# Output projection beside the last HGRN2 head: eight tiles over half of the k-tiles, in place of two tiles over all of them

## The chip, the core and the metric

The kernel runs on one core of one Trainium2 chip. The metric is the device time of one execution, in microseconds. The kernel before takes 3098.37 us (median of 3 runs, 3093.49 to 3100.5).

## What is computed

One decoder layer and a final RMSNorm, for a prompt of 16 meta tokens and 512 tokens, and for 8 sample sequences of 8 tokens (`D_MODEL` 2048, `d_ff` 8192). The parts that matter here:

```
proj = rmsnorm(x) @ w_in                       # 8208 columns, for both head groups
og   = gated DeltaNet, 8 heads (short conv, l2norm, delta rule, head norm, gate)
oh   = HGRN2, 8 heads (state expansion 128):
         f = lb + (1 - lb) * sigmoid(fh);  k = 1 - f
         S_t = diag(f_t) S_{t-1} + k_t v_t^T ;  o_t = S_t^T q_t   (chunks; head norm, gate)
mix  = concat(og, oh)                          # 2048 columns, 128 per head
x    = x + mix @ w_out                         # the output projection and its residual
x    = x + relu(rmsnorm(x) @ w_up)^2 @ w_down
y    = rmsnorm(x)
```

The outputs are y for both groups, and the new conv, DeltaNet and HGRN2 states.

## The kernel before, in words

**Layout.** Activations lie transposed: 128 features on the partitions, tokens along the free dimension (592 = 64 sample + 16 meta + 512 prompt; behind the mixers 576, as two halves of 288). A product of 2048 features is a sum over 16 k-tiles. Each FP32 operand is split into a high part in fp32r (a copy on ScalarE) and a low part (the difference, on VectorE), and a k-tile is three products (high x high, low x high, high x low) of two halves: six matmuls (`ktile`, line 877; its line in the trace is 882). A weight *unit* is eight k-tiles of one output tile (128 x 1024 FP32, 512 KB). It is loaded by SyncE's queue into one of four slots of `w_raw` (`load`, line 490), split by `hi` on ScalarE (A at line 1317) and by `lo` on VectorE (line 1767) into one of two slots of `w_hi` and `w_lo`. A load waits until the low half of the unit four earlier is made; a high half until the unit two earlier is multiplied. Output tiles alternate between two PSUM buffers (`outs`, line 378); a tile may start when the one two earlier has been evacuated (`s_evac`).

**Heads.** For each of the eight heads TensorE runs 16 units of the input projection, and between its k-tiles stages of the mixers: in the first half the HGRN2 stages of the head before, in the second half the DeltaNet stages of this head. So the last HGRN2 head has no input projection left to run beside. Its stages come in the order of `HG_STAGES`: gdn_out, gates, gates_b, turn_v, turn_k, stw, diag, seven levels l1 to l64, o, out, st0. Each engine has its own queue and takes them in this order:

- TensorE (`hg`, line 1091): turn_v and turn_k are transposes (the helper's line is 958), stw the state products (lines 1113 and 1115), diag the diagonal scores (1119), a level 8 or 10 small matmuls (1127), o the outputs (1134 to 1140), out the head norm's sums (942), st0 the sample state (1144).
- VectorE (`hg`, line 2020): gates_b makes the decayed keys `kd` (2048), the first level's argument (1988, 1989) and the products `qe` (2051) and `zs` (2053); turn_k copies the turned keys (2062) and forms the level's operands `q` and `kk` (1998, 1999); stw makes the carried states (2066, 2070); a level takes the scores of the level before (2018, preceded by a one-element instruction of line 145), forms its operands and the argument of the next level but one. Levels wait for each other through these.
- ScalarE (`hg`, line 1463) makes the exponential of each argument (1461).
- GpSimd stores the HGRN2 sample state when VectorE has made its sum (2090), at the very end of the head.

**The output projection before.** Its operands are the 16 heads' outputs, one per k-tile. Fourteen are read back from DRAM (`mix_scratch`) and split one by one between the stages (`split_hi`, line 1529, run at 1540; `split_lo`, line 2158, run at 2168); the DeltaNet output of the last head (k = 7) and the HGRN2 output of the last head (k = 15) are split from SBUF (1535, 1536; 2165, 2166). `K_ORDER` starts with 7 and ends with 15; `SPLITS` says behind which stage each split stands, on ScalarE and VectorE alike. TensorE's queue is filled by a table written by hand: `fill` names the k-tiles that `out_k` (line 1185) issues behind each stage, each for two output tiles:

```
fill = {"turn_v": (0,), "diag": (1, 2), "l1": (3, 4), "l2": (5, 6), "l4": (7,), "l32": (8, 9), "l64": (10,), "o": (11,),
        "out": (12,), "st0": (13, 14)}
```

The k-tile 15 follows, and then the other 14 tiles, one after the other, two units each. `out_evac` (line 2178, run at 2191) adds a tile's residual to PSUM and writes `x1`. That memory is the heads' working memory, so the first one waits for all state stores (`s_hst_out` the last of them), and the low halves of later weights are queued behind it on VectorE. The residual of tiles 0 and 1 is loaded before into `res01`, in the memory of the conv input `u`; that of the other tiles is loaded into `x1` itself, in twelve transfers from `xT_scratch` (lines 544 to 546), when the state stores have landed. Behind each tile GpSimd stores it (line 798) and sums its square (804), ScalarE squares (1557) and scales it (1561), and both split engines prepare the forms for the MLP, whose matmuls (line 1229) follow.

## Time and profile before

| | us |
|---|---|
| median of 3 runs | 3098.37 |
| the profiled execution's own time | 3107.0 |
| its span, first to last instruction | 3105.2 |
| TensorE matmuls busy | 2993.0 (96%) |
| VectorE busy | 2031.0 (65%) |
| ScalarE busy | 1202.5 (39%) |
| GpSimd busy | 319.2 (10%) |
| mean granted TensorE clock | 0.981 |

### The profile page before, as it was taken

How to read it: one execution, taken by the hardware profiler on the slowest of the kernel's cores; microseconds unless marked ns; L12 is line 12 of the kernel's file. 1: busy time of each engine (PE TensorE's matmuls, PEld its weight loads, DVE VectorE, ACT ScalarE, POOL GpSimd, SP SyncE). 2: the span in 40 equal slices, each digit the busy share in tenths (PEclk: the TensorE clock that was granted, in tenths of full speed). 3: DMA queues.
4: the chain of work that ended last, by engine and by line, in shares of the span. 5: the costliest groups of instructions: out<-in, count | busy, mean ns of one | idle time of the engine just before them, and what ended most of it. 6: DMA issues, size and time to landing. Idle time of an engine off the chain costs nothing.

```text
span 3105.2 us, 52468 instructions
## 1 busy us (share of the span) xinstructions
PE 2993.0 (96%) x22024; PEld 2936.3 (95%) x22024; DVE 2031.0 (65%) x2820; ACT 1202.5 (39%) x1522; POOL 319.2 (10%) x433
## 2 busy tenths in 40 slices
PE   7999999999999999978999999999998999999998
PEld 7999999999999999978998999999997999999998
DVE  5546463637464655644448777777778887878885
ACT  4323333323333333333334444444445444444454
POOL 5010101011101011010110000000000000000011
PEclk9999999999999999988999999999999999999999
DMA  7233563433232333334334444444458666666665
GB/s 208 57 77 65 72 67 53 83 59 78 63 74 62 77 64 74 66 111 119 105 101 127 144 153 142 155 141 157 137 161 265 194 194 196 192 196 193 193 196 186
DMA packets 513500, 392.61 MB, mean 126 GB/s; under 512 B 16401, under 2 KB 483041, under 8 KB 513265
## 3 DMA queue, kind: packets, MB, share of 16 engines
q1 hardware_dynamic: 461664, 268.86, 35.1%
q0 software_dynamic: 22832, 88.39, 7.9%
q10 hardware_dynamic: 28768, 32.00, 3.6%
q8 instruction: 174, 2.85, 0.4%
q14 instruction: 62, 0.50, 0.1%
HBM read 304.87 MB, written 84.33 MB: 125 GB/s over the span
## 4 chain that ended last, share of the span: by engine, by line
PE 86%; DVE 8%; ACT 2%; issue 2%; DMA 1%; POOL 0%; DVEq 0%; ACTq 0%; POOLq 0%
PE main L1229 38%; PE main L882 28%; PE mx L1229 6%; PE mx L1127 2%; PE mx L1026 1%; PE mx L1034 1%; PE mx L958 1%; PE mx L942 1%; DVE w_lo L1767 1%; PE mx L985 1%; DVE tmp L1875 1%; PE mx L993 1%; PE mx L1068 1%; PE mx L1134 0%; PE mx L1062 0%
## 5 line engine op out<-in xcount | busy, mean ns | idle before, releaser
L882 PE MATMUL main<-h_hi,w_hi 128*128 128x296 f32 (+1 forms) x2592 | 620.0, 321 | 12.4 <-DVE w_lo L1767 9.1
L1229 PE MATMUL main<-forms_a,w_hi 128*128 128x288 f32 x3072 | 615.6, 296 | 9.9 <-DVE forms_a L2344 6.0
L1229 PE MATMUL main<-forms_b,w_hi 128*128 128x288 f32 x3072 | 613.9, 295 | 7.2 <-DVE forms_b L2344 5.0
L882 PE MATMUL main<-h_lo,w_hi 128*128 128x296 f32 (+1 forms) x2592 | 573.8, 303 | 0.0
L882 PE MATMUL main<-h_hi,w_lo 128*128 128x296 f32 (+1 forms) x2592 | 572.2, 303 | 0.0
L1229 PEld LDWEIGHTS main<-forms_a,w_hi 128*128 128x128 f32 x3072 | 494.8, 189 | 11.0 <-issue 10.8
L1229 PEld LDWEIGHTS main<-forms_b,w_hi 128*128 128x128 f32 x3072 | 492.1, 188 | 8.6 <-issue 5.6
L1229 PE MATMUL main<-forms_a,w_lo 128*128 128x288 f32 x1536 | 455.3, 296 | 0.0
L1229 PE MATMUL main<-forms_b,w_lo 128*128 128x288 f32 x1536 | 452.2, 294 | 0.0
L882 PEld LDWEIGHTS main<-h_hi,w_hi 128*128 128x128 f32 x2592 | 423.7, 194 | 25.4 <-DVE w_lo L1767 10.0
L882 PEld LDWEIGHTS main<-h_lo,w_hi 128*128 128x128 f32 x2592 | 431.4, 193 | 0.0
L882 PEld LDWEIGHTS main<-h_hi,w_lo 128*128 128x128 f32 x2592 | 430.3, 193 | 0.0
L1614 ACT ACTIVATE w_hi<-w_raw 128x1024 fp32r<-128x1024 f32 x256 | 271.3, 1060 | 331.2 <-PE main L1229 224.0
L2291 DVE TENSOR_TENSOR w_lo<-w_raw,w_hi 128x1024 fp32r<-128x1024 f32 x256 | 312.3, 1220 | 65.3 <-PE main L1229 65.3
L1614 ACT ACTIVATE w_hi<-w_sum 128x1024 fp32r<-128x1024 f32 x190 | 201.5, 1061 | 297.3 <-PE main L1229 297.2
L1229 PEld LDWEIGHTS main<-forms_a,w_lo 128*128 128x128 f32 x1536 | 289.2, 188 | 0.0
L1229 PEld LDWEIGHTS main<-forms_b,w_lo 128*128 128x128 f32 x1536 | 289.1, 188 | 0.0
L1317 ACT ACTIVATE w_hi<-w_raw 128x1024 fp32r<-128x1024 f32 x162 | 170.5, 1052 | 298.0 <-PE main L882 297.9
L1767 DVE TENSOR_TENSOR w_lo<-w_raw,w_hi 128x1024 fp32r<-128x1024 f32 x162 | 197.7, 1221 | 115.6 <-ACT w_hi L1317 115.6
L2291 DVE TENSOR_TENSOR w_lo<-w_sum,w_hi 128x1024 fp32r<-128x1024 f32 x190 | 234.1, 1232 | 16.6 <-PE main L1229 16.6
L1229 PE MATMUL mx<-forms_b,w_hi 128*128 128x288 f32 x1024 | 206.9, 296 | 2.5 <-DVE forms_b L2344 1.7
L1229 PEld LDWEIGHTS mx<-forms_b,w_hi 128*128 128x128 f32 x1024 | 164.3, 188 | 3.0 <-issue 3.0
(382 smaller groups left out, 3617.6 us busy)
## 6 DMA issues: line engine op xcount, KB each, us to landing
w_raw<-in_w_in SPq DMA_DIRECT2D x130, 512.0 KB, 8.1
w_raw<-in_w_up SPq DMA_DIRECT2D x128, 512.0 KB, 4.1
w_raw<-in_w_down SPq DMA_DIRECT2D x100, 512.0 KB, 4.5
u_forms<-ub POOLq DMA_DIRECT2D x32, 1152.0 KB, 6.7
z<-x_scratch SPq DMA_DIRECT2D x32, 576.0 KB, 7.5
x_scratch<-z POOLq DMA_DIRECT2D x31, 576.0 KB, 3.1
stage<-u_forms ACTq DMA_DIRECT2D x30, 576.0 KB, 4.0
w_raw<-in_w_out SPq DMA_DIRECT2D x32, 512.0 KB, 3.9
```

The source lines that it names most:

```text
L882: ins = mm(out[:, half, :], w[:, ring, k, :], x[:, kx, half * width:half * width + width], start=first and n == 0, stop=last_ and n == 2)
L942: ins = mm(mx[:, i + half, 0:HALF], ones[:, :], src[:, half * HALF:half * HALF + HALF], start=True, stop=True)
L958: ins = pe.transpose(mxf[:, 512 * i + n_ * P:512 * i + n_ * P + P], src(c), ident[:, :])
L985: ins = mm(mx[:, 2 * i + half, 0:HALF], ones[0:16, :], sel[i][:, half * HALF:half * HALF + HALF], start=True, stop=True)
L993: ins = mm(mxf[:, 512 * i + c * P:512 * i + c * P + P], win(qkv[:, 1, :], c), win(right, c), start=True, stop=True)
L1026: ins = mm(bank(0, 64 * c, 64), xl[:, c, :], left, start=True, stop=True)
L1127: ins = mm(bank(i % 2, 64 * c, 64), win(hkk, c), hqq[:, ctok(c):ctok(c) + 64], start=True, stop=True)
L1229: ins = mm(out, w[:, k, :], x[:, kx, :], start=i in (0, 1, 3) and k == 0 and n == 0, stop=k == KP - 1 and n == 2, skip_group_check=True)
L1317: A(w_hi[:, ring % 2], w_raw[:, ring], ACT.Copy).then_inc(s_hi, 1)
L1614: A(hi_slot(u_), src, ACT.Copy).then_inc(s_hi, 1)
L1767: TT(w_lo[:, ring % 2], w_raw[:, ring], w_hi[:, ring % 2].bitcast(F32), ALU.subtract).then_inc(s_lo, 1)
L2291: TT(w_lo[:, u_ % 2], src, hi_slot(u_).bitcast(F32), ALU.subtract).then_inc(s_lo, 1)
```

## The change

The output projection is cut differently. Its tile steps q are now 24: q = 0 to 7 are the output tiles 0 to 7 over the k-tiles 0 to 7 (the DeltaNet heads), one unit each; q = 8 to 15 are the same tiles over the k-tiles 8 to 15; q = 16 to 23 are the tiles 8 to 15 over all 16. The k-tiles are issued in this order from one generator, and `FILL_TO` says how many steps of a k-tile have been issued behind each stage. An early tile's evacuation adds its half sum to its residual in SBUF (`early_part`, in memory that the last head does not use any more), and the later one adds the other half and writes `x1`. Six early evacuations, and the weight halves of the units 2 to 7, stand behind the stages of `EARLY_AT` on VectorE and ScalarE. On ScalarE a stage's weight half comes ahead of its splits, on VectorE behind them. The residuals of the tiles 0 to 7 are loaded in 24 small transfers between the first two and the last two groups of mixer rows, those of the tiles 8 to 15 in the twelve transfers behind the state stores. The splits stand behind other stages, and the products `qe` and `zs` move on VectorE from gates_b to the end of diag. In the diff, hunks that only renumber waits are left out.

```diff
@@ -68,8 +68,13 @@
...
 BLOCK_AT = [2, 3, 0, 1, 4, 5]
-SPLITS = {"gdn_out": (0,), "gates_b": (2,), "turn_v": (3,), "turn_k": (4,), "stw": (5,), "diag": (6,), "l1": (7,), "l2": (8,),
-          "l4": (9,), "l16": (10,), "l32": (11,), "l64": (12,), "o": (13, 14), "out": (15,)}
+SPLITS = {"gdn_out": (0,), "gates": (1,), "gates_b": (2,), "turn_k": (3,), "stw": (4, 5), "diag": (6,), "l1": (7,), "l4": (8,),
+          "l8": (9,), "l16": (10,), "l32": (11,), "l64": (12,), "o": (13, 14), "out": (15,)}
+EARLY = 8
+EARLY_AT = {"l2": 0, "l4": 1, "l16": 2, "l64": 3, "o": 4, "out": 5}
+FILL_TO = {"turn_v": 3, "turn_k": 4, "diag": 7, "l1": 12, "l2": 17, "l4": 22, "l8": 26, "l16": 30, "l32": 34, "l64": 39, "o": 45,
+           "out": 54, "st0": 71}
+PART_AT = [(0, 288), (11520, 288), (576, 288), (1152, 288), (10592, 288), (12200, 288), (12776, 288), (11168, 2184)]
@@ -94,9 +99,14 @@
-def out_done(m):
-    return OUT_U0 + (3 + m if m < 2 else 2 * m + 2)
+def last_unit(q):
+    return q if q < 2 * EARLY else 2 * (q - EARLY) + 1
+def out_done(q):
+    return OUT_U0 + last_unit(q) + 1
@@ -195,8 +205,8 @@
...
 LEVEL_DVE = [s for i, b in enumerate(LEVELS[1:]) for s in ([f"a{LEVELS[i]}", f"q{b}", f"kk{b}"] + ([f"arg{2 * b}"] if b < 64 else []))]
-HG_DVE = (["clamp", "zclamp", "g", "b", "k0", "k", "kdarg", "kd", "arg1", "qe", "zs", "vx", "kdt", "q1", "kk1", "arg2", "sc_0"]
-          + [f"sc_{c}" for c in range(1, NW)] + ["diag"] + LEVEL_DVE + ["a64"]
+HG_DVE = (["clamp", "zclamp", "g", "b", "k0", "k", "kdarg", "kd", "arg1", "vx", "kdt", "q1", "kk1", "arg2", "sc_0"]
+          + [f"sc_{c}" for c in range(1, NW)] + ["diag", "qe", "zs"] + LEVEL_DVE + ["a64"]
@@ -246,6 +256,9 @@
...
+        with ExitStack() as s:
+            part_mem = sb("part_mem", [P, 15536], stack=s)
@@ -318,7 +331,10 @@
-        res01 = u[:, :, :].rearrange("p a b -> p (a b)")[:, 0:2 * TN].rearrange("p (a b) -> p a b", a=2)
+        def early_part(m):
+            o, step = PART_AT[m]
+            return part_mem[:, o:o + 2 * step].rearrange("p (a n) -> p a n", a=2)[:, :, 0:TH]
@@ -375,8 +391,8 @@
...
-        def outs(m):
-            return main[(OUT_T0 + m) % 2][:, :, 0:TH]
+        def outs(q):
+            return main[(OUT_T0 + q) % 2][:, :, 0:TH]
@@ -512,7 +528,7 @@
             def out_load(v):
-                m, k0 = (v % 2, UK * (v // 2)) if v < 4 else (v // 2, UK * (v % 2))
+                m, k0 = (v % EARLY, UK * (v // EARLY)) if v < 2 * EARLY else (v // 2, UK * (v % 2))
@@ -521,15 +537,35 @@
...
             raw = h_lo[:, :, :].bitcast(F32)
-            for i, (k0, k1) in enumerate(MIX_GROUPS):
+            def mix_load(i):
+                k0, k1 = MIX_GROUPS[i]
...
+            def early_residual(m):
+                part_ = early_part(m)
+                done = s_res[0 if m < 2 else 1]
+                sp.dma_start(part_[:, 0, 0:NS], xT_dram[:, m, 0:NS]).then_inc(done, 16)
+                sp.dma_start(part_[:, 0, NS:TH], xT_dram[:, m, T0:NM + TH]).then_inc(done, 16)
+                sp.dma_start(part_[:, 1, :], xT_dram[:, m, NM + TH:N]).then_inc(done, 16)
+            mix_load(0)
+            mix_load(1)
...
             gdve.wait(sp, "last", HEADS - 1)
-            sp.dma_start(res01[:, :, 0:NS], xT_dram[:, 0:2, 0:NS]).then_inc(s_res, 16)
-            sp.dma_start(res01[:, :, NS:TN], xT_dram[:, 0:2, T0:N]).then_inc(s_res, 16)
-            for v in range(4, 8):
+            gdve.wait(sp, "y", HEADS - 1)
+            sp.wait_ge(s_gsc_out, 16 * HEADS)
+            early_residual(0)
+            early_residual(1)
+            out_load(4)
+            out_load(5)
+            for m in range(2, EARLY):
+                early_residual(m)
+            mix_load(2)
+            mix_load(3)
+            for v in range(6, 11):
@@ -538,13 +574,13 @@
...
             sp.wait_ge(s_hsc_out, 16 * HEADS)
-            for i, (k0, k1) in enumerate(((1, 2), (2, KP))):
+            for i, (k0, k1) in enumerate(((4, 5), (5, KP))):
...
                     sp.dma_start(x1_half(j, 1)[:, k0:k1, :], xT_dram[:, rows, NM + TH:N]).then_inc(s_xT[i], 16)
-            for v in range(8, 2 * KT):
+            for v in range(11, 2 * KT):
@@ -1182,36 +1218,38 @@
...
                 head(h, False)
-            def out_k(n):
-                k = K_ORDER[n]
-                pe.wait_ge(s_k_lo, KT + n + 1)
-                for m in range(2):
-                    u_ = OUT_U0 + 2 * (n // UK) + m
-                    if n % UK == 0:
-                        pe.wait_ge(s_lo, u_ + 1)
-                    if n == 0:
-                        pe.wait_ge(s_evac, OUT_T0 + m - 1)
-                    ins = ktile(outs(m), u_ % 2, k % UK, k, n == 0, n == KT - 1, TH)
-                    if n % UK == UK - 1:
-                        ins.then_inc(s_unit, 1)
-            fill = {"turn_v": (0,), "diag": (1, 2), "l1": (3, 4), "l2": (5, 6), "l4": (7,), "l32": (8, 9), "l64": (10,), "o": (11,),
-                    "out": (12,), "st0": (13, 14)}
+            def out_step(q, v, k, first, last_, unit_end):
+                if q in (0, EARLY):
+                    pe.wait_ge(s_k_lo, KT + K_ORDER.index(k) + 1)
+                u_ = OUT_U0 + v
+                ins = ktile(outs(q), u_ % 2, k % UK, k, first, last_, TH)
+                if unit_end:
+                    ins.then_inc(s_unit, 1)
+            def out_tile(q):
+                m, vs = (q, [q]) if q < 2 * EARLY else (q - EARLY, [2 * (q - EARLY), 2 * (q - EARLY) + 1])
+                k0 = UK if EARLY <= q < 2 * EARLY else 0
+                ks = K_ORDER[0:UK] if q == 0 else list(range(k0, k0 + UK * len(vs)))
+                for i, k in enumerate(ks):
+                    v = vs[i // UK]
+                    if i % UK == 0:
+                        pe.wait_ge(s_lo, OUT_U0 + v + 1)
+                    if i == 0:
+                        pe.wait_ge(s_evac, OUT_T0 + q - 1)
+                    out_step(q, v, k, i == 0, i == len(ks) - 1, i % UK == UK - 1)
+                    yield
+            early = (step for q in range(EARLY + KT) for step in out_tile(q))
+            filled = 0
...
                 hg(st, HEADS - 1, None)
-                for n in fill.get(st, ()):
-                    out_k(n)
-            out_k(KT - 1)
-            for v in range(4, 2 * KT):
-                m = v // 2
-                pe.wait_ge(s_lo, OUT_U0 + v + 1)
-                if v % 2 == 0:
-                    pe.wait_ge(s_evac, OUT_T0 + m - 1)
-                for k in range(UK):
-                    ins = ktile(outs(m), v % 2, k, UK * (v % 2) + k, v % 2 == 0 and k == 0, v % 2 == 1 and k == UK - 1, TH)
-                ins.then_inc(s_unit, 1)
+                while filled < FILL_TO.get(st, 0):
+                    next(early)
+                    filled += 1
+            for step in early:
+                pass
@@ -1542,16 +1580,14 @@
...
                 hg(st, HEADS - 1)
-                if st == "gates":
-                    split_hi(1)
+                if st in EARLY_AT:
+                    u_ = OUT_U0 + EARLY_AT[st] + 2
+                    hi(u_, u_ % RAW)
...
                     split_hi(n)
-                if st in ("l8", "l16"):
-                    u_ = OUT_U0 + (2 if st == "l8" else 3)
-                    hi(u_, u_ % RAW)
             def square(m):
-                act.wait_ge(s_evac, OUT_T0 + m + 1)
+                act.wait_ge(s_evac, OUT_T0 + EARLY + m + 1)
@@ -1577,16 +1613,16 @@
...
                 elif k == "b":
-                    act.wait_ge(s_evac, OUT_T0 + KT)
+                    act.wait_ge(s_evac, OUT_T0 + EARLY + KT)
...
-            for v in range(4, 2 * KT):
+            for v in range(EARLY, 2 * KT):
...
                 for m in range(KT):
-                    at_v = 4 if m == 0 else 2 * m + 3
+                    at_v = last_unit(EARLY + m) + 2
@@ -2047,10 +2083,6 @@
...
                     level_arg(0, h)
-                    W(hact, "eb")
-                    done(TT(hqe, hq[:, :], heb, ALU.mult), "qe")
-                    W(hact, "zsig")
-                    done(TT(hz[:, :], hz[:, :], ho[:, :], ALU.mult), "zs")
@@ -2074,6 +2106,10 @@
...
                     done(dve.copy_predicated(ha, imask[:, :, :], wins(2)), "diag")
+                    W(hact, "eb")
+                    done(TT(hqe, hq[:, :], heb, ALU.mult), "qe")
+                    W(hact, "zsig")
+                    done(TT(hz[:, :], hz[:, :], ho[:, :], ALU.mult), "zs")
@@ -2167,28 +2203,38 @@
...
-            for st in HG_STAGES:
-                hg(st, HEADS - 1, None)
-                for n in SPLITS.get(st, ()):
-                    split_lo(n)
-                if st in ("l8", "l16"):
-                    u_ = OUT_U0 + (2 if st == "l8" else 3)
-                    lo(u_, u_ % RAW)
-            def out_evac(m):
+            def out_evac(q):
+                dve.wait_ge(s_unit, out_done(q))
+                if q < EARLY:
+                    if q == 0:
+                        dve.wait_ge(s_res[0], 96)
+                    if q == 2:
+                        dve.wait_ge(s_res[1], 48 * (EARLY - 2))
+                    TT(early_part(q), outs(q), early_part(q), ALU.add).then_inc(s_evac, 1)
+                    return
+                m = q - EARLY
                 if m == 0:
-                    dve.wait_ge(s_res, 32)
+                    dve.wait_ge(s_evac, OUT_T0 + EARLY)
...
                     dve.wait_ge(s_hsc_out, 16 * HEADS)
-                if m == 2:
+                if m == EARLY:
                     dve.wait_ge(s_xT[0], 96)
-                if m == 4:
+                if m == EARLY + 2:
                     dve.wait_ge(s_xT[1], 96)
-                dve.wait_ge(s_unit, out_done(m))
-                TT(x1_tile(m), outs(m), two(res01[:, m, :]) if m < 2 else x1_tile(m), ALU.add).then_inc(s_evac, 1)
+                TT(x1_tile(m), outs(q), early_part(m) if m < EARLY else x1_tile(m), ALU.add).then_inc(s_evac, 1)
+            for st in HG_STAGES:
+                hg(st, HEADS - 1, None)
+                if st != "gates":
+                    for n in SPLITS.get(st, ()):
+                        split_lo(n)
+                if st in EARLY_AT:
+                    q = EARLY_AT[st]
+                    out_evac(q)
+                    lo(OUT_U0 + q + 2, (OUT_U0 + q + 2) % RAW)
```

## Rows read from the trace of the kernel before

**Rows 1.** The page: the chain that ended last, by engine.
```profile
PE 86%; DVE 8%; ACT 2%; issue 2%; DMA 1%; POOL 0%; DVEq 0%; ACTq 0%; POOLq 0%
```

**Rows 2.** Busy time by stretch; columns as in the first line.
```profile
core 0: us, PE busy (x) PEld busy (x) DVE busy (x) ACT busy (x) POOL busy (x), PEclk, DMA share, GB/s
1367.40:1447.10 79.70, 51.73 (x335) 48.03 (x333) 49.80 (x96) 31.10 (x50) 5.80 (x13) 0.81 0.33 103
1374.80:1392.60 17.80, 8.15 (x36) 7.41 (x37) 14.51 (x26) 10.30 (x18) 0.00 (x0) 0.52 0.75 234
1392.60:1408.60 16.00, 16.00 (x127) 15.71 (x125) 12.29 (x29) 3.60 (x7) 1.15 (x2) 1.00 0.02 5
1408.60:1447.10 38.50, 25.43 (x164) 23.71 (x163) 18.26 (x35) 12.14 (x20) 2.14 (x5) 0.82 0.16 46
1447.10:1627.10 180.00, 180.00 (x1345) 180.00 (x1346) 82.08 (x95) 55.93 (x80) 32.43 (x29) 0.99 0.44 129
```

**Rows 3.** TensorE's waits, 1366 to 1450 us: total, times, longest, in us.
```profile
PE mx L1127 <- DVE tmp L1999: 7.5, 2, 3.8
PE main L882 <- DVE w_lo L1767: 5.6, 1, 5.6
PE mx L958 <- DVE tmp L2048: 5.5, 1, 5.5
PE mx L1113 <- DVE tmp L2062: 4.1, 1, 4.1
PE main L882 <- DVE h_lo L2166: 3.3, 1, 3.3
```

**Rows 4.** TensorE's timeline: start, us, line, operation, count, idle time before it.
```profile
1375.98 0.69 PE L882 MATMUL main<-h_hi,w_hi 128*128 128x288 f32 x2
...
1383.13 1.33 PE L958 MATMUL mx<-ident,tmp 128*128 128x128 f32 x5 [5.51 <-DVE tmp L2048]
1388.60 0.80 PE L1113 MATMUL mx<-tmp 128*128 128x128 f32 x2 [4.14 <-DVE tmp L2062]
...
1395.90 1.22 PE L1127 MATMUL mx<-tmp 128*128 128x64 f32 x10
...
1434.85 1.88 PE L1144 MATMUL mx<-tmp 128*128 128x512 f32 x4
```

**Rows 5.** VectorE's timeline.
```profile
1385.12 0.75 DVE L2168 TENSOR_TENSOR h_lo<-h_lo,h_hi 128x576 fp32r<-128x576 f32 x1
...
1387.72 0.82 DVE L2062 COPY tmp<-mx 128x640 f32<-128x640 f32 x1
...
1392.19 0.28 DVE L2066 COPY tmp<-mx 128x128 f32<-128x128 f32 x1
...
1395.42 1.40 DVE L2168 TENSOR_TENSOR h_lo<-h_lo,h_hi 128x576 fp32r<-128x576 f32 x2
...
1401.74 0.86 DVE L2018 COPY_PREDICATED tmp<-pmask,mx 128x320 f32<-128x320 uint8 x1
...
1405.36 0.76 DVE L2168 TENSOR_TENSOR h_lo<-h_lo,h_hi 128x576 fp32r<-128x576 f32 x1 [1.28 <-ACT h_hi L1540]
...
1409.70 1.22 DVE L1767 TENSOR_TENSOR w_lo<-w_raw,w_hi 128x1024 fp32r<-128x1024 f32 x1 [1.64 <-ACT w_hi L1317]
...
1446.94 0.75 DVE L2191 TENSOR_TENSOR x<-main,u 128x576 f32<-128x576 f32 x1
```

**Rows 6.** ScalarE's timeline: an exponential and a weight's high half.
```profile
1408.09 0.63 ACT L1461 ACTIVATE tmp<-tmp 128x512 f32<-128x512 f32 x1 [2.76 <-DVE tmp L1989]
1408.63 1.04 ACT L1317 ACTIVATE w_hi<-w_raw 128x1024 fp32r<-128x1024 f32 x1
```

**Rows 7.** The chain of waits in order of time: start, us, what.
```profile
1440.97 3.84 DMA out_hgrn_sample<-hstate
```

**Rows 8.** SyncE's queue (first two), and DMA issues, 1444 to 1465 us (the last).
```profile
1444.96 0.34 SPq L544 DMA_DIRECT2D x<-xT_scratch  x1
...
1455.62 1.56 SPq L494 DMA_DIRECT2D w_raw<-in_w_out  x1
w_raw<-in_w_out SPq DMA_DIRECT2D x4, 512.0 KB, 9.6
```

More of the change, by code:

```diff
@@ L423, in hymba_kernel @@
         s_mixin = [sem(f"mix_loaded{i}") for i in range(4)]
-        s_res = sem("residual01_loaded")
+        s_res = [sem(f"early_residual_loaded{i}") for i in range(2)]
         s_xT = [sem(f"residual_loaded{i}") for i in range(2)]
@@ L794, in _ @@
             for m in range(KT):
-                pool.wait_ge(s_evac, OUT_T0 + m + 1)
+                pool.wait_ge(s_evac, OUT_T0 + EARLY + m + 1)
                 if m >= 2:
@@ L1237, in product_waits @@
                     if p < 2:
-                        pe.wait_ge(s_evac, OUT_T0 + KT - 1 + p)
+                        pe.wait_ge(s_evac, OUT_T0 + EARLY + KT - 1 + p)
                     else:
@@ L2221, in token_form @@
                 elif n == 2:
-                    dve.wait_ge(s_evac, OUT_T0 + KT) if last_ else dve.wait_ge(s_xs, 2 * k + 2)
+                    dve.wait_ge(s_evac, OUT_T0 + EARLY + KT) if last_ else dve.wait_ge(s_xs, 2 * k + 2)
                     dve.wait_ge(s_flo, form_no(f"1_{k}"))
@@ L2230, in token_form @@
                 ins.then_inc(s_tf, 1)
-            for v in range(4, 2 * KT):
-                for m in range(KT - 1):
-                    if v == (4 if m == 0 else 2 * m + 3):
-                        out_evac(m)
+            for v in range(EARLY, 2 * KT):
+                for q in range(EARLY + KT - 1):
+                    if v == last_unit(q) + 2:
+                        out_evac(q)
                 lo(OUT_U0 + v, (OUT_U0 + v) % RAW)
                 for m in range(KT):
-                    at_v = 4 if m == 0 else 2 * m + 3
+                    at_v = last_unit(EARLY + m) + 2
                     k = m // 2
@@ L2390, in _ @@
             form_lo("1_7")
-            out_evac(KT - 1)
+            out_evac(EARLY + KT - 1)
             mlp_lo(0, 1)
```

## The prediction

> **What bounds the kernel now.** The page comes first: TensorE is 86% of the chain that ended last [rows 1]. So time is won only where TensorE stands still, or works at the lower of its two clock levels. The second view cuts the region of the change into stretches. From 1447.1 to 1627.1 us TensorE is busy for all 180.00 us: 224 k-tiles (six matmuls each) at 0.80 us. Before that lie the 79.7 us in which the last HGRN2 head runs, and there TensorE is busy for only 51.73 [rows 2]. The third view names the waits in these 28.0 us: 3.3 for the first operand's low half, 5.5 for the decayed keys, 4.1 for their turned copy, 7.5 in two waits of the late levels, 5.6 for weights queued behind the store of the HGRN2 state [rows 3]; 2.0 are left for short ones at the head's start. The last thing to see is the granted clock: 0.52 in 1374.8 to 1392.6, 0.82 from 1408.6 on [rows 2]. At 0.5 (1.2 GHz) a pair of matmuls takes 0.69 us and the next starts after 0.48 [rows 4], so a k-tile costs 1.44 us and not 0.80. With 8.15 and 25.43 us of busy time in these stretches, the share lost to it is 0.48 x 8.15 + 0.18 x 25.43 = 8.5, about 9 us. The change can win at most about 37 us.
>
> **What the change does to the work.** The k-tiles stay 256, and so does their time. Before, 26 are issued ahead of the head's last matmuls (stage st0); after, 54. They come from eight tiles over the first eight k-tiles, whose operands exist early; the two old tiles needed all sixteen. Added are 8 evacuations on VectorE (24 in place of 16), 0.68 us each from start to start (0.75 in the row) [rows 5]. Moved into the head are four more pairs of weight halves: 0.97 us on ScalarE (1.04 in the row), 1.14 on VectorE (1.22) [rows 5, 6]. The products qe and zs go from before the first turn to after the diagonal; they stood just ahead of the split at 1385.12 and took 0.69 each, like it.
>
> **The walk up to level 1**, in the times of the profiled execution. Up to 1375 nothing differs. Step 2 needs the low half that started at 1385.12 [rows 5]; without qe and zs it starts at 1383.7 and ends at 1384.4. At the slow clock step 2 ends at 1385.9, and only then does TensorE reach the turn of the keys, which it ran at 1383.13 [rows 4]. It takes 1.3, so their copy on VectorE starts at 1387.2, where it was 1387.72.
> Step 3 is queued ahead of the state products (stw), and needs the fourth split, which ScalarE makes behind the level-2 exponential. Before, the same sequence (copy, products, argument, exponential, split) took from 1387.72 to 1392.19 [rows 5], 4.5 us; now it ends at 1391.7. Step 3 costs 1.44, so stw starts at 1393.1, where it was 1388.60 [rows 4].
> stw takes 2.0 at the slow clock and frees VectorE at 1395.1. From the first state copy to the end of the diagonal it then needed 3.2 us with one split (1392.19 to 1395.42 [rows 5]); now there are two (3.9), then qe and zs (1.4) and split six (0.7), end at 1401.1. Step 6 waits for that last split and stands ahead of level 1: 1401.9, where it was 1395.90 [rows 4], **6.0 us late**.
>
> **From level 1 to st0.** Before, this took 38.95 us (1395.90 to 1434.85 [rows 4]): 20 k-tiles at 0.80 (16.0), 7.5 idle, and 15.5 for the matmuls of the stages with the slow clock. Of the 4.6 us that the slow clock took from 1408.6 on, some 3.5 fall into this stretch, so the stages alone are 12.0. After, there are 47 k-tiles (37.6) and the same 12.0. Whether idle time is left is decided by VectorE's and ScalarE's loop per level. A plain level runs from 1401.74 to the end of the split at 1405.36 + 0.67 [rows 5], 4.3 us. TensorE's own share is 4.0 to 5.0 (four or five k-tiles and the level's matmuls), so these are covered. At l4, l16 and l64 both weight halves and an evacuation stand in the loop too: 0.97, 1.14 and 0.68 more, about 7.1 us. The slack of the levels between takes most of it up; I keep 2.0 us idle, at level 32. The sum is 37.6 + 12.0 + 2.0 = 51.6: st0 at 1453.5, **18.7 us late**. I take the clock to stay up, since the two late waits of 3.8, behind which it fell before, are filled.
>
> **After st0.** 28 k-tiles fewer are left: 28 x 0.80 = 22.4 us. The wait of 5.6 goes: the state's store starts 6.1 us behind st0 (1434.85 to 1440.97 [rows 4, 7]) and takes 3.84, so it lands at 1463.4. Meanwhile TensorE has steps 54 to 79, none of which needs the memory it frees: 26 x 0.80 = 20.8 us, to 1475.8. Were this cover gone, the 5.6 would come back. The slow start behind that wait goes too, 3 k-tiles at 0.64 more, 1.9 us. Together **29.9 us** are won.
>
> **Sum:** 29.9 - 18.7 = **11 us won**. The rest of the program follows TensorE and shifts as a whole.
>
> **Queues.** SyncE's queue now issues 24 small residual loads ahead of the last two groups of mixer rows. Before, twelve went out in 10.7 us (1444.96 to 1455.62), and a load behind them landed after 9.6 [rows 8]. Twice that issue time, 21 us from 1375, and 9.6 bring the last mixer rows by 1406; they are due at level 4, near 1412. The second residual group is due at about 1423. I cost both at nothing, with 6 us of cover on the worst reading. Behind the state's store, twelve loads precede the weights of unit 11. At the old prices these are there at 1463.4 + 10.7 + 9.6, their halves 2.1 later, 1485.9; step 88 is due at 1482.2. The loads are 8 tiles now and not 14; by that ratio it is 1477. I take 0, between 0 and 4 us lost. Stores and squares now come every 6.4 us for eight tiles, where a tile took 12.8. For a tile VectorE worked 82.08 / 14 = 5.9 us and ScalarE 4.0 [rows 2], with two weight units each; with one it is 4.7 and 3.0, under 6.4. Taken as 0, at most 1 us.
>
> **Bounds.** The level-1 delay ends above at 9 us, if the clock stays low over the fill behind it (five k-tiles at 0.64 more), and below at 4, if the splits wait less. Idle time in the levels is 0 to 6 us (2.0 in each long level). So the mechanism as walked gives 11 - 3.2 - 4.0 = 4 to 11 + 2.0 + 2.0 = 15 us.
>
> **Rivals.**
> **A, the clock stays low.** It rose after stw, the diagonal and some k-tiles had run without a gap from 1388.60; the next stretch is at 1.00 throughout [rows 2]. In the new order this work has gaps, about 0.8 before step 4 and 1.9 before step 6. If the clock comes back only when level 1's fill has run, steps 4 to 11 cost 0.64 more each (5.1) and level 1 0.9: the gain is 5, or 3 with one more idle level. For it speaks that the stretch with gaps stood at 0.52; against it, that nearly all of the time from 1401 on is busy.
> The Trainium skill, page "TensorE: Matmul & The Clock Gate", section "The HAM clock gate (the "warmup" mystery)", says "the default state is throttled, and activity releases the throttle". By that rule work with gaps releases it later than work without, which is this rival and its 3 to 5 us. The trace agrees in direction (0.52 with gaps, 1.00 without).
> **B, the loop of VectorE and ScalarE becomes the bound: slower.** The place is the six periods from level 1 to level 64. TensorE needs 27 k-tiles (21.6) and 5.7 of level matmuls there (about 1.0 for ten [rows 4], 0.8 for eight), 27.3 us. If every period took the long loop's 7.1, that is 42.6: 15.3 more. The gaps bring the slow clock for some five k-tiles, 3.2. Against 11 + 2.0 won (the idle time counted above is inside it) the kernel is 5.5 us slower, and 7 or more with the clock low for longer. It decides from a mean period of (27.3 + 13) / 6 = 6.7 us. For it speaks that this loop ended the late waits (7.5 [rows 3]) and that a weight half waited 1.64 for ScalarE [rows 5]; against it, that only three levels carry the extra work.
> **C, more is won.** The new k-tiles fall into gaps only, and no stage is delayed. TensorE's work without slow clock (52 - 9) and only 10 us of early waits would end 27 us sooner; half way there, the gain is 19. Against it: fills stand ahead of stage matmuls in one queue, in order.
> **D, it does not do what it says:** nothing is hidden, and every added k-tile pushes st0 back by its own length. That is 28 x 0.80 + 6.0 = 28.4 us of delay against 29.9: 1.5 won. Against it stand the 7.5 us of late waits, which must be filled first.
>
> **How the numbers follow.** The profiled execution took 3107.0 us, 8.6 above the median of 3098.37 (3093.49 to 3100.5); its span is 3105.2. The gain is a difference within that execution, so I take it off the median: 3098.4 - 11 = **3087 us**. Chances: as walked 0.60; A 0.19; C 0.09; B 0.06; D 0.06. A measurement of this kernel can tell about 0.2%, 6.2 us, from no change. Faster by more are the walk, C and 0.04 of A: 0.73. Within it lie the rest of A (0.15), half of D and 0.01 of B: 0.19. Slower by more are the rest of B, with the clock low for longer, and of D, with a late transfer on top: 0.08. The range leaves out B, the worse half of D and the far part of C: gains of 1 to 21 us, 3077 to 3097.
>
> **What would show it.** In the changed trace, level 1's matmuls start near 1402 and st0 near 1454. TensorE has no wait on the HGRN2 state's store, waits of about 21 us between 1367 and 1460 (28.0 before), and a clock at 1.00 from about 1400. From st0 to the first MLP matmul there are 202 k-tiles without a gap, and that matmul comes near 1616, where it was 1627.1. Wrong would be: level periods near 6.7 us with waits on w_lo or h_lo (B); the clock at 0.5 past 1405 (A); st0 later than 1460 (D); ScalarE waiting for mixer rows, or TensorE for weights near step 88 (the queue).

## The result, and the profile after

After the change the kernel takes 3072.39 us (median of 4 runs, 3069.9 to 3074.89), against 3095.93 (4 runs, 3093.49 to 3100.5) for the kernel before on the same chip. The ratio is 0.992, with a 95% interval of 0.9904 to 0.9935. So 23.5 us are won by the medians, about twice the 11 that were forecast, and the time lies below the forecast range of 3077 to 3097. The profiled execution of the kernel after took 3074.89 us. The page of the kernel after (its head and the chain by engine):

```profile
span 3073.1 us, 52508 instructions
...
PE 86%; DVE 8%; ACT 3%; issue 2%; DMA 1%; POOL 0%; DVEq 0%; ACTq 0%; POOLq 0%
```

Read against [rows 1], the chain tells nothing: the shares are the same but for one point of ScalarE's. What helps is to set the two traces side by side at the same places and to ask where the distance between them grows. The places are stw (the first state product of an HGRN2 head) of heads 1 and 7, the turn of the values of the last head (where the region of the change begins), and the first MLP matmul. TensorE's timeline, kernel before (its first MLP matmul starts at 1627.08):

```profile
218.96 0.80 PE L1113 MATMUL mx<-tmp 128*128 128x128 f32 x2 [2.89 <-DVE tmp L2062]
1222.46 0.79 PE L1113 MATMUL mx<-tmp 128*128 128x128 f32 x2 [2.88 <-DVE tmp L2062]
1370.72 0.77 PE L958 MATMUL mx<-ident,hv 128*128 128x128 f32 x5 [0.84 <-ACT tmp L1453]
```

The same places in TensorE's timeline of the kernel after:

```profile
216.78 0.49 PE L1149 MATMUL mx<-tmp 128*128 128x128 f32 x2 [1.52 <-DVE tmp L2094]
1203.23 0.49 PE L1149 MATMUL mx<-tmp 128*128 128x128 f32 x2 [1.51 <-DVE tmp L2094]
1348.77 0.77 PE L994 MATMUL mx<-ident,hv 128*128 128x128 f32 x5 [0.84 <-ACT tmp L1491]
1596.52 0.43 PE L1267 MATMUL main<-forms_a,w_hi 128*128 128x288 f32 x2
```

| stretch | before | after | won |
|---|---|---|---|
| start to stw of head 1 | 218.96 | 216.78 | 2.2 |
| stw of head 1 to stw of head 7 | 1003.50 | 986.45 | 17.1 |
| on to the turn of the values, last head | 148.26 | 145.54 | 2.7 |
| **the region of the change**, to the first MLP matmul | 256.36 | 247.75 | 8.6 |
| MLP and end of the span | 1478.1 | 1476.6 | 1.5 |

Of the 32.1 us between the two spans, 22 are won before the region that the prediction walked even begins. (The profiled execution of the kernel before was a long one, 3107.0 against a median of 3095.93, so the 32.1 overstate the 23.5.) The region itself gives 8.6, near the 11 forecast.

**What happens in the earlier heads.** TensorE's waits, kernel before, all of 0 to 1366 us:

```profile
PE mx L1113 <- DVE tmp L2062: 22.1, 7, 4.3
```

and kernel after, 0 to 1353 us:

```profile
PE mx L1149 <- DVE tmp L2094: 13.8, 7, 4.2
```

It is one wait per head, of the state products for the copy of the turned keys. What stands ahead of that copy is seen in VectorE's timeline of the kernel before, head 1:

```profile
213.50 0.77 DVE L2051 TENSOR_TENSOR tmp<-hq,tmp 128x592 f32<-128x592 f32 x1
214.18 0.77 DVE L2053 TENSOR_TENSOR hz<-hz,ho 128x592 f32<-128x592 f32 x1
214.87 1.35 DVE L2058 TENSOR_TENSOR tmp<-tmp,seq_rows 128x1152 f32<-128x1152 f32 x1
...
216.95 1.21 DVE L1767 TENSOR_TENSOR w_lo<-w_raw,w_hi 128x1024 fp32r<-128x1024 f32 x1
218.08 0.82 DVE L2062 COPY tmp<-mx 128x640 f32<-128x640 f32 x1
```

The first two rows are the products qe and zs. The stage function in which the change moves them serves all eight heads, not the last one alone. Without them the copy comes 1.4 us sooner in six of the seven heads, and the wait of 2.89 becomes 1.52. Head 3 is the exception: its wait is 4.34 before and 4.23 after. There VectorE itself stands still ahead of the third row, the product of L2058, until a store of the DeltaNet output has landed: for 1.36 us before, and after, with the two products gone, for 2.62 us. VectorE's timeline of the kernel after, head 3:

```profile
542.86 1.36 DVE L2090 TENSOR_TENSOR tmp<-tmp,seq_rows 128x1152 f32<-128x1152 f32 x1 [2.62 <-DMA mix_scratch<-tmp]
```

The clock follows. Here are the 30 us around stw (10 ahead of it, 20 behind) of heads 1, 2, 3 and 7, kernel before (heads 4 and 6 are like 2, head 5 is like 1); columns are the window, its length, TensorE's busy time and matmuls, the granted clock, the DMA share, GB/s:

```profile
208.96:238.96 30.00, 27.11 (x189) 0.89 0.34 76
376.94:406.94 30.00, 27.11 (x211) 1.00 0.68 91
544.85:574.85 30.00, 25.66 (x183) 0.89 0.64 106
...
1212.46:1242.46 30.00, 27.12 (x189) 0.89 0.38 82
```

and heads 1 and 3 of the kernel after (2 and 4 to 7 are at 1.00 like 1):

```profile
206.78:236.78 30.00, 28.48 (x221) 1.00 0.44 99
536.95:566.95 30.00, 25.77 (x188) 0.94 0.63 106
```

Before, the clock fell in four of seven heads: in head 3, whose wait is 4.34, and in three others whose wait is 2.9. Such a window has 22 matmuls fewer (189, not 211). After, with 1.5 (in head 6 about 2.0) of wait, it stayed up behind stw everywhere but in head 3, whose wait is 4.23.

These windows show only a part of the low clock in the earlier heads. From stw of head 1 to 20 us behind stw of head 7 TensorE's granted clock stood at 0.5 for 58 us before and for 24 us after. Of the 34 us less, 24 lie at the stw stages (27 before, 3 after) and 10 elsewhere in the heads (31 before, 21 after), where the change moves nothing. A k-tile takes 1.44 us at this clock and not 0.80, so at most about half of such time is lost, and less where TensorE waits anyway.

**The region** gives, in TensorE's timeline of the kernel after:

```profile
1360.31 0.85 PE L918 MATMUL main<-h_hi,w_hi 128*128 128x288 f32 x2 [5.59 <-DVE h_lo L2204]
1364.21 1.27 PE L994 MATMUL mx<-ident,tmp 128*128 128x128 f32 x5
...
1371.72 0.63 PE L1149 MATMUL mx<-tmp 128*128 128x128 f32 x2
...
1380.76 1.22 PE L1163 MATMUL mx<-tmp 128*128 128x64 f32 x10
...
1406.60 1.26 PE L1163 MATMUL mx<-tmp 128*128 128x64 f32 x8 [2.14 <-DVE tmp L2035]
...
1408.24 0.68 PE L918 MATMUL main<-h_lo,w_hi 128*128 128x288 f32 x2
...
1433.85 1.88 PE L1180 MATMUL mx<-tmp 128*128 128x512 f32 x4
```

From the turn of the values (1370.72 before, 1348.77 after), in us:

| | before | forecast | after |
|---|---|---|---|
| turn of the keys | 12.41 | 15.2 | 15.44 |
| stw | 17.88 | 22.4 | 22.95 |
| level 1 | 25.18 | 31.2 | 31.99 |
| st0 | 64.13 | 82.8 | 85.08 |
| first MLP matmul | 256.36 | 245.4 | 247.75 |

The windows of the kernel after: two parts of the region ahead of st0, then st0 to the first MLP matmul.

```profile
1380.70:1406.50 25.80, 23.76 (x188) 1.00 0.14 41
1406.50:1433.85 27.35, 27.25 (x198) 0.94 0.20 59
1433.85:1596.50 162.65, 162.65 (x1218) 1.00 0.44 127
```

Behind st0 there is no gap any more; the wait of 5.6 for weights [rows 3] is gone.

### The profile page after: what moved, and what is told of

Same layout as the page of the kernel before. It is cut to its first block, busy times and chain, and to the rows that moved or that the text cites. A ratio compares the mean times of both kernels' runs of the same rounds, so it can differ in the third digit from the quotient of the medians.

```text
span 3073.1 us, 52508 instructions
## 1 busy us (share of the span) xinstructions
PE 2974.0 (97%) x22024; PEld 2918.8 (95%) x22024; DVE 2032.5 (66%) x2828; ACT 1202.3 (39%) x1522; POOL 316.9 (10%) x433
## 4 chain that ended last, share of the span: by engine, by line
PE 86%; DVE 8%; ACT 3%; issue 2%; DMA 1%; POOL 0%; DVEq 0%; ACTq 0%; POOLq 0%
PE main L1267 38%; PE main L918 27%; PE mx L1267 6%; PE mx L1163 2%; PE mx L1062 1%; PE mx L1070 1%; PE mx L994 1%; PE mx L978 1%; DVE w_lo L1803 1%; DVE tmp L1911 1%; PE mx L1021 1%; PE mx L1029 1%; PE mx L1104 1%; PE mx L1170 0%; PE mx L1098 0%
## 5 line engine op out<-in xcount | busy, mean ns | idle before, releaser
L918 PE MATMUL main<-h_hi,w_hi 128*128 128x296 f32 (+1 forms) x2592 | 617.0, 320 | 21.8 <-DVE h_lo L2204 13.8
L2350 DVE TENSOR_TENSOR z<-z,main 128x288 f32<-128x288 f32 x192 | 87.2, 454 | 119.8 <-PE main L1267 119.7
```

Source lines behind the costliest of these rows:

```text
L918: ins = mm(out[:, half, :], w[:, ring, k, :], x[:, kx, half * width:half * width + width], start=first and n == 0, stop=last_ and n == 2)
L2350: TT(o[:, q, :], o[:, q, :], src, ALU.add).then_inc(s_ev, 1)
```

## The experiments

Two theories stood after the result. **Every head:** the move of qe and zs acts in all eight heads, through the shorter wait and the clock behind it. **The region:** the out-projection's new order is worth more than 11 us, and the earlier start is the chance of one execution. Kernels that were measured together share their runs of the kernel before. Gains in us below are one minus the ratio, times the median of those runs.

**The move alone (b_qezs): before, with qe and zs moved.** They go from behind the level's argument to behind the diagonal's predicated copy; the list of VectorE's steps is changed to match.

```diff
 level_arg(0, h)
-W(hact, "eb")
-done(TT(hqe, hq[:, :], heb, ALU.mult), "qe")
-W(hact, "zsig")
-done(TT(hz[:, :], hz[:, :], ho[:, :], ALU.mult), "zs")
...
 done(dve.copy_predicated(ha, imask[:, :, :], wins(2)), "diag")
+W(hact, "eb")
+done(TT(hqe, hq[:, :], heb, ALU.mult), "qe")
+W(hact, "zsig")
+done(TT(hz[:, :], hz[:, :], ho[:, :], ALU.mult), "zs")
```

> The kernel before, with nothing changed but the place of the products qe and zs on VectorE (from gates_b to the end of diag), in all eight heads, since the stage is shared. Theory 1 (the shared stage): the wait ahead of the state products shrinks from 2.9 to about 1.5 us in seven heads, and the clock stays at 1.00 behind it: 1.4 us of wait and about 1.3 us of slow matmuls for each head. The time falls by 13 to 20 us, ratio 0.993 to 0.996. Rival theory 2 (all of the gain comes from the output projection beside the last head): at most 3 us, ratio 0.999 or more.

**All but the move (a_qezs_back): after, with qe and zs put back.** The same lines the other way, so that only the output projection is changed.

> The changed kernel with qe and zs put back to gates_b in all heads, so that only the output projection is changed. Theory 1: the gain over the kernel before is the one that I had predicted for the output projection, about 10 us (8 to 13), ratio 0.9955 to 0.9975; the waits of 2.9 us ahead of the state products are back. Theory 2: the gain stays at 20 us or more, ratio 0.9935 or less.

**Half of the move (b_zs): before, with only zs moved, to the same place.**

```diff
 done(TT(hqe, hq[:, :], heb, ALU.mult), "qe")
-W(hact, "zsig")
-done(TT(hz[:, :], hz[:, :], ho[:, :], ALU.mult), "zs")
...
 done(dve.copy_predicated(ha, imask[:, :, :], wins(2)), "diag")
+W(hact, "zsig")
+done(TT(hz[:, :], hz[:, :], ho[:, :], ALU.mult), "zs")
```

> The kernel before with only zs moved, so that the wait ahead of the state products is about 2.2 us in the seven heads. If the gain is the length of the wait alone, it is half of that of moving both. If the clock is the larger part and is lost only behind a longer wait, most of the gain is there already (ratio within 0.001 of that with both moved); if the clock still falls behind 2.2 us, only 5 us are won (ratio 0.9985).

**The wait shortened from TensorE's side (b_stw22): before, VectorE's and ScalarE's order untouched.** Two more steps of the projection that TensorE runs between the stages stand ahead of stw, one more ahead of diag.

```diff
-HG_STAGES = {"gdn_out": 2, "gates": 3, "conv_in": 6, "gates_b": 9, "turn_v": 10, "turn_k": 18, "stw": 20, "diag": 22,
+HG_STAGES = {"gdn_out": 2, "gates": 3, "conv_in": 6, "gates_b": 9, "turn_v": 10, "turn_k": 18, "stw": 22, "diag": 23,
```

> The kernel before with the stages stw and diag two and one k-tiles later in TensorE's order (positions 22 and 23 in place of 20 and 22), and VectorE's and ScalarE's work untouched. Theory 1: two k-tiles of 0.82 us fill the wait of 2.9 us, which becomes about 1.3 us in seven heads, and the clock stays up. The gain is like that of moving qe and zs: 12 to 20 us, ratio 0.9935 to 0.996. The last head is not touched by it (its order has no positions). Rival: VectorE's own queue is what counts (qe and zs delay all that follows), then nothing is won, ratio 1.000, and the wait turns up at level 1.

These four ran together (before: 3098.8 us, 15 runs). "Six periods" is the time from stw of head 1 to stw of head 7 in the profiled execution.

| kernel | median us | ratio (95%) | won, us | stw wait, heads 1 to 7 | six periods |
|---|---|---|---|---|---|
| before | 3098.8 | | | 22.1 | 1003.50 |
| b_qezs | 3083.76 | 0.9944 (0.9931 to 0.9957) | 17 | 14.3 | 987.65 |
| a_qezs_back | 3085.43 | 0.9956 (0.9941 to 0.9971) | 14 | 22.5 | 996.64 |
| b_zs | 3093.36 | 0.9982 (0.9972 to 0.9991) | 6 | 18.4 | 997.41 |
| b_stw22 | 3076.61 | 0.9924 (0.9909 to 0.9939) | 24 | 11.3 | 982.23 |

The move alone wins 17 us, with the out-projection as it was before. Its last head gives next to nothing of this: from the turn of the values to the first MLP matmul it took 255.9 us, where before took 256.36. Without the move the new order wins 14 (interval 9 to 18), and its region took 248.1 us: 8.3 less. So both parts are real, and the forecast of 11 was about right for the second. The rest of the 14 lies outside the region, if it is more than noise: the six periods of a_qezs_back are 6.9 us shorter than those of before, with the same waits and less low clock (see the last section). The sum of the two parts, 31, is above the 25 of both together, but each figure is good to 4 us only.

The rows behind it, windows around stw as above. Heads 1 and 3 of b_qezs:

```profile
204.67:234.67 30.00, 28.50 (x220) 1.00 0.44 97
535.45:565.45 30.00, 25.26 (x180) 0.89 0.65 102
```

Heads 1, 2 and 4 of b_zs, whose wait is 2.20 us in each of them:

```profile
207.87:237.87 30.00, 27.80 (x204) 0.94 0.40 87
372.54:402.54 30.00, 27.80 (x216) 1.00 0.70 96
706.30:736.30 30.00, 27.80 (x205) 0.94 0.39 89
```

and TensorE's timeline of b_stw22, head 1:

```profile
215.04 0.49 PE L1113 MATMUL mx<-tmp 128*128 128x128 f32 x2 [1.24 <-DVE tmp L2062]
```

In b_zs the clock still fell in five of the seven heads: in 1, 4 and 5 with a wait of 2.20, in 6 with 2.65, in 3 with 4.80; but the windows have 0.94 and not 0.89. In b_qezs it fell in head 3 alone. In b_stw22 the products qe and zs stand where they stood; only the wait is shorter, and it wins 24 us, more than the move itself and more than the 12 to 20 expected of it. So a shorter wait is enough, wherever the two products stand. That it wins more fits its waits, which are 11.3 us in all and not 14.3. The region theory falls with b_qezs, which has the old output projection, and with the 8.3 us of a_qezs_back's region.

The time at the clock of 0.5, in us, from stw of head 1 to 20 us behind stw of head 7, one profiled execution each:

| kernel | at the stw stages | elsewhere in these heads | together |
|---|---|---|---|
| before | 27 | 31 | 58 |
| b_zs | 17 | 24 | 41 |
| a_qezs_back | 14 | 20 | 34 |
| b_qezs | 7 | 20 | 27 |
| b_stw22 | 3 | 17 | 20 |
| b_warm (below) | 7 | 10 | 17 |

**The clock by itself (b_warm): before, with three matmuls that nothing reads put into the wait, heads 1 to 7.** The order of the real work is not changed.

```diff
 hpe.done(turns(2, lambda c: win(hkd, c), range(NW)), "turn_k")
+if next_first is not None:
+    W(hact, "vt")
+    for _ in range(3):
+        mm(bank(0, 0, 512), ident[:, :], masks[:, 0:4, :], start=True, stop=True)
```

> The kernel before with three extra matmuls of 512 columns between the turn of the keys and the state products, in the first seven heads, into a PSUM bank that nothing reads; they lie in the wait of 2.9 us (about 0.66 us each) and nothing else is moved. Theory 1 (part of the loss is the clock and not the wait): the state products start no earlier behind the turn of the keys, but run at 1.00, and the time falls by what the clock cost alone, 6 to 12 us, ratio 0.996 to 0.998. If only the length of the waits counted, the time stays (ratio 1.000), and if the extra matmuls stick out of the wait it rises.

Measured: 3085.87 us (before 3098.69, 9 runs), ratio 0.9956 (0.9943 to 0.997), a little more than expected. TensorE's timeline of head 1, kernel before (stw itself is shown above, at 218.96):

```profile
213.72 0.71 PE L958 MATMUL mx<-ident,tmp 128*128 128x128 f32 x5
...
224.22 1.68 PE L1119 MATMUL mx<-hq,tmp 128*128 128x128 f32 x10
```

and of b_warm:

```profile
210.71 0.71 PE L958 MATMUL mx<-ident,tmp 128*128 128x128 f32 x5
211.26 2.74 PE L1112 MATMUL mx<-masks,ident 128*128 128x512 f32 x6
215.95 0.49 PE L1117 MATMUL mx<-tmp 128*128 128x128 f32 x2 [0.33 <-DVE tmp L2066]
...
218.82 1.28 PE L1123 MATMUL mx<-hq,tmp 128*128 128x128 f32 x10
```

The turn of the keys to stw takes 5.24 us in both: the real work waits as long as it did (in head 3 longer, 7.80 and not 6.69). But from stw to the diagonal it is 2.87 us and not 5.26. The windows around stw of heads 1 and 3:

```profile
205.95:235.95 30.00, 29.67 (x217) 1.00 0.41 84
537.29:567.29 30.00, 27.12 (x176) 0.89 0.73 101
```

Work that computes nothing wins 14 us (interval 9 to 18), and the six periods are 991.07 and not 1003.50. So the clock alone, with no wait made shorter, is worth that much. This does not depend on one execution: the mean granted clock of its five executions was 0.985 to 0.989, that of the nine of before 0.978 to 0.985. The table above adds that only half of the low clock that went was at stw; the other half went elsewhere in the heads, for a reason that was not tried.

It does not follow that the clock is most of what the move wins, for b_warm has less low clock than b_qezs. For b_qezs the rows give this: of the 15.9 us of its six periods, 6.5 are shorter ways from the turn of the keys to stw, and 9.4 are left for the clock, whose low time within them fell by 24 us (at most 12 us of loss). By the medians it is 17, of which 7.8 are wait and 9 are left (5 to 13). Wait and clock are thus about equal parts.

The Trainium skill, page "TensorE: Matmul & The Clock Gate", section "The HAM clock gate (the "warmup" mystery)", says that activity releases the throttle. This run agrees: activity alone, of no use to the result, brought the windows of heads 1, 5 and 7 from 0.89 to 1.00. Head 3 stayed at 0.89, with 2.88 us of wait left.

**Is there more to win with the clock after the move (b_qezs_warm)?** b_qezs with two such matmuls in its wait of 1.5 us; `range(2)` in the edit above.

> The kernel before with qe and zs moved and with two extra matmuls of 512 columns in the wait of 1.5 us that is left ahead of the state products in seven heads. If moving qe and zs has already kept the clock up, there is nothing left for the extra matmuls to win but in the third head, whose wait is 4.7 us: the ratio is within 0.001 of that with the two products moved (0.9944). If it falls by as much as in the kernel before (0.0044), the clock was not what moving them had won.

Measured: 3085.73 us (before 3097.03, 11 runs), ratio 0.9961 (0.9948 to 0.9975), where b_qezs had 0.9944 (0.9931 to 0.9957). That is 0.0017 off, outside the 0.001 expected, but the intervals overlap. No gain is seen, and little was left behind stw: b_qezs has the low clock there in head 3 alone.

**Two versions that go on from the kernel after.** a_stw22 has stw at step 22 and diag at 23, as b_stw22. a_fill3 changes the last head alone: the fourth early k-tile, whose low half is late, is issued behind the turned keys' products and not ahead of them. a_both has both edits.

```diff
-FILL_TO = {"turn_v": 3, "turn_k": 4, "diag": 7, "l1": 12, "l2": 17, "l4": 22, "l8": 26, "l16": 30, "l32": 34, "l64": 39, "o": 45,
+FILL_TO = {"turn_v": 3, "stw": 4, "diag": 7, "l1": 12, "l2": 17, "l4": 22, "l8": 26, "l16": 30, "l32": 34, "l64": 39, "o": 45,
```

> The changed kernel with stw and diag at positions 22 and 23 in the first seven heads as well. The wait of 1.5 us ahead of the state products is filled by two k-tiles of 0.82 us. If waits below the length at which the clock falls cost only themselves, 7 x 1.4 = 10 us are won over the changed kernel: ratio 0.988 to 0.990 to the kernel before. Rival: the wait moves to level 1, since VectorE's work between stw and level 1 (carried states, diagonal, qe, zs: about 4 us) now has 2 k-tiles less to hide behind; then 0 to 4 us are won, ratio 0.991.

> The changed kernel with the fourth early k-tile behind the state products and not ahead of them, in the last head only. By my walk this k-tile held the state products back by some 4 us. If that is what makes level 1 late, stw starts 4 us earlier and level 1 some 2 us earlier, for VectorE still has the fourth split ahead of the first state copy: ratio lower than that of the changed kernel by 0.0005, hardly to be told by the times, but to be seen in the start of level 1 behind the turn of the values (32.0 us in the changed kernel). Rival: nothing moves, since the fourth and the seventh split set level 1.

> Both edits of the two runs before together, as a candidate for the fastest version: the sum of their gains, ratio 0.988 to 0.991 to the kernel before.

These ran beside b_warm (before 3098.69):

| kernel | median us | ratio (95%) | won, us |
|---|---|---|---|
| a_stw22 | 3065.38 | 0.9891 (0.9878 to 0.9905) | 34 |
| a_fill3 | 3068.94 | 0.9902 (0.9889 to 0.9916) | 30 |
| **a_both** | **3061.76** | **0.988** (0.9866 to 0.9893) | 37 |

TensorE's waits of a_stw22, 190 to 1380 us:

```profile
PE mx L1163 <- DVE tmp L2035: 4.5, 7, 0.7
...
PE mx L1149 <- DVE tmp L2094: 3.0, 2, 2.6
```

The wait for the turned keys is left in head 3 (2.6) and for 0.3 us in head 6; small new ones of 0.6 stand at level 1 of each head. In a_fill3, TensorE's timeline of the last head:

```profile
1346.03 1.20 PE L994 MATMUL mx<-ident,hv 128*128 128x128 f32 x5 [0.85 <-ACT tmp L1491]
1363.65 0.80 PE L1149 MATMUL mx<-tmp 128*128 128x128 f32 x2 [0.92 <-DVE tmp L2094]
...
1375.24 1.22 PE L1163 MATMUL mx<-tmp 128*128 128x64 f32 x10
```

stw comes 17.6 us after the turn of the values, where the kernel after needed 22.95, and level 1 after 29.2, where it needed 31.99. This is the 5 us of delay that the walk had found in the queue's order (the late fourth k-tile stands ahead of stw); 2.8 us of it remain won at level 1. The time of a_fill3 can't be told from that of the kernel after (0.992, 0.9904 to 0.9935). a_both beats both kernels of the case.

**The last head's clock (a_both_warm).** a_both with five unread matmuls behind the first early k-tile, and four behind the turn of the keys, in the last head.

```diff
 filled += 1
+if filled == 1:
+    for _ in range(5):
+        mm(bank(3, 0, 512), ident[:, :], masks[:, 0:4, :], start=True, stop=True)
...
```

> The version with both edits, and in the last head nine extra matmuls of 512 columns that nothing reads: five behind the first early k-tile (a wait of 5.6 us at the slow clock follows it) and four behind the turn of the keys. They change no order and no wait; they only keep TensorE busy. If the slow clock from the turn of the keys to the diagonal (0.5 in that stretch) is lost to these waits, stw, diag and the k-tiles between run at 1.00, and 2 to 4 us are won over the version with both edits (ratio 0.9868 to 0.9875 to the kernel before). If the extra matmuls stick out of the waits, or the chain of splits on VectorE sets the end whatever the clock, nothing is won or up to 2 us are lost.

Measured: 3060.41 us (before 3097.03), ratio 0.9887 (0.9873 to 0.9901), against 0.988 (0.9866 to 0.9893) of a_both: no gain in the times, and the ratio of 0.9868 to 0.9875 that was expected was missed. A gain of 2 us could not be told by them. TensorE's timeline of a_both_warm, the turn of the values of the last head and level 1:

```profile
1334.92 0.77 PE L994 MATMUL mx<-ident,hv 128*128 128x128 f32 x5 [0.84 <-ACT tmp L1498]
...
1361.90 1.22 PE L1167 MATMUL mx<-tmp 128*128 128x64 f32 x10
```

Level 1 comes 27.0 us after the turn of the values, where a_both needs 29.0, and from the turn to the first MLP matmul it is 242.8 us and not 244.8. So 2.0 us are won in this region of one execution, the low end of what was expected. Behind the first early k-tiles TensorE still waits for low halves: 3.4 us once, then 2.9 in three waits. That these splits on ScalarE and VectorE keep the rest from being won is likely, but no run shows it.

## Why the prediction was wrong, point by point

**The step that failed** is the accounting of the moved products, in "Up to 1375 nothing differs". The move was costed as an edit of the last head (the split of 1385.12 earlier, the diagonal later by 1.4), although the lines lie in the stage function that all heads run. The bound "at most about 37 us" has the same fault: it counts the last head's region only. In place of nothing, the move gave 17 us (b_qezs; 13 to 21), nearly all in the seven earlier heads, since the last head's region gained 0.5. By the rows of b_qezs the waits became 22.1 - 14.3 = 7.8 us shorter, in the kernel after 22.1 - 13.8 = 8.3. The rest, about 9 us, goes with the low clock in these heads, behind the waits and elsewhere, which the prediction had looked for in the last head only. That the clock alone can win time in these heads is shown by b_warm (14 us). A sharp split between the two can't be had, since a shorter wait is also what keeps the clock up. The row of 22.1 us over seven heads would have shown in the waits of the whole span; the prediction took them from 1366 us on only [rows 3].

**The walk held.** The turn of the keys, stw and level 1 came 0.2, 0.6 and 0.8 us later than forecast. The long wait came at step 2, for the low half (5.59 us), and the late fourth split held up stw (a wait of 4.6 us), as walked. In all, TensorE stood still for 19.4 us from the turn of the values to st0; about 21 had been forecast for nearly the same stretch.

**Level 1 to st0** was forecast at 51.6 us and took 53.1. The idle time kept at level 32 was 2.0; it measured 2.14. But "I take the clock to stay up" was wrong for the stretch behind this wait: pairs of matmuls at 1408 us took 0.68, the length at the low clock [rows 4], and the window has 0.94. That and the 0.8 at level 1 are the 2.3 us by which the region's 8.6 miss the 11.

**After st0** the forecast was right: 162.65 us without a gap, 202 k-tiles at 0.80, the wait on the state's store gone. The queue cost nothing. SyncE's queue of the kernel after, the first of 24 residual loads and the first mixer row behind them, then the first of the twelve later ones and the weights behind these:

```profile
1351.30 0.34 SPq L549 DMA_DIRECT2D part_mem<-xT_scratch  x1
...
1364.99 0.43 SPq L543 DMA_DIRECT2D h_lo<-mix_scratch  x1
...
1441.19 0.34 SPq L580 DMA_DIRECT2D x<-xT_scratch  x1
...
1447.75 49.77 SPq L510 DMA_DIRECT2D w_raw<-in_w_out  x11
```

The 24 went out in 13.7 us, not 21, and the twelve in 6.6, not 10.7.

**The rivals.** A (the clock stays low) did not come: from stw to level 1 the window already has 0.91 with 5.87 us of work, about 0.5 us lost, and from 1380.70 on it has 1.00. B (the loop of VectorE and ScalarE becomes the bound) did not come: from 1380.70 to 1406.50 TensorE is busy for 23.76 of 25.80 us. C (more is won in the region) did not come either: the time was below the range through another place. D (nothing is hidden) did not come, since 28 more k-tiles delayed st0 by 21.0 us and not by 28.4.

## What to carry to other kernels

Before an edit is costed, ask how often its lines run: a line in a helper acts in every iteration, and the waits of the whole span, grouped by line, show what it touches there. A wait of TensorE can have two prices, its own length and the low clock behind it. Here they were about equal, and with the waits shortened from 2.9 to 1.5 us the low clock behind them was gone. Such a wait can be shortened from either side, by less work ahead of it on the engine waited for or by more work ahead of it on the one that waits. Here the second won more, and it also left less wait (11.3 us against 14.3).

## What the runs showed of the hardware

- In this kernel a TensorE wait of 2.9 us was followed by a low clock in three of the five heads that have it (1, 5 and 7; not 2 and 4), one of 2.2 us in three of the same five, one of 1.2 to 1.5 in none. So the length alone doesn't decide; what else does was not tried. These are single executions, with seven heads each.
- The same wait did not have the same price in every kernel. In a_qezs_back, whose waits are those of the kernel before, one of these five heads (head 4, 0.94) had the low clock, and head 6 with its wait of 3.33 had it too (0.94), where before it had not. Its last head began 11.3 us earlier (1359.41, not 1370.72). So the profiled execution of the kernel before had the low clock more often than these waits always bring, which is probably part of why the two spans differ by 32.1 us and the medians by 23.5.
- The clock falls in a second place of each period too, in a stretch that the change doesn't touch. Windows between heads 4 and 5, kernel before and then after, each in its own fence:

```profile
793.05:804.93 11.88, 11.78 (x73) 0.77 0.26 48
```

```profile
782.15:793.84 11.69, 11.59 (x76) 0.85 0.25 53
```

  At about 11.7 us of work these are 2.7 and 1.7 us lost. Over all heads such places hold more of the low clock than the stw stages do, in every kernel of the table above. Why they differ from kernel to kernel was not tried.
- Three matmuls of 512 columns that nothing reads, put into each of seven waits, made the kernel 0.44% faster.
- The wait of head 3 is long in every kernel (2.6 to 4.8 us) because VectorE, ahead of the copy of the turned keys, waits there for a store of the DeltaNet output to land: for 1.36 us before, 2.62 after, 3.14 in b_qezs. In the other heads this wait isn't there. So moving the two products could win nothing in head 3. Why the store lands late in this head was not tried.
